# Another order of twelve matrix products: both column halves under one stationary operand, and a tile waited for and released whole

## The chip, the core and the metric

The kernel runs on one core of a Trainium2 chip. The metric is the device time of one execution in microseconds. The kernel before takes 2241.05 us, the median of three runs (2237.48 to 2243.5).

## The reference, cut to what matters

Two transformer layers over 256 tokens of width 1024: an attention mixer, and then a retrieval of experts. The expert part is where the change lies. For each token 8 heads choose 16 of 16384 experts each, and then

```
a   = gelu(sum_d u[e, d] * h[t, d]) * gate[t, e]      # for the chosen experts e of token t
out = sum_e a[t, e] * v[e, :]                         # 256 tokens x 1024
```

The kernel gathers nothing. It computes the product with all 16384 experts, 128 tiles of 128 experts, and the gate is zero where an expert was not chosen. So each layer has an upward pass (h with every tile of `u`) and a downward pass (the weighted activations with every tile of `v`). All of it is in 32-bit floats.

## The kernel before, in words

To keep 32-bit accuracy with TensorE's reduced format, each operand X is split into a high part and a rest, X = hi + lo, and a product is made of three: hi\*hi, hi\*lo, lo\*hi. The work around one tile j of the downward pass is divided so:

- SyncE brings 512 KB of `v` into `raw`, a ring of four (`load_v`, L292), and the 128 KB of stored activations back into `back`, a ring of four that lies in `wmod_ring` (`fetch`, L302). It waits for `lo_done` of the tile four back, and for `al_done` of the tile three ahead of the fetch's own.
- ScalarE makes `hi` of the tile in two instructions, one for each half of 512 columns (`split`, L745), and then `a_hi` of the activations (`split_a`, L773). `hi`, `lo`, `a_hi` and `a_lo` are rings of two, so tile j+2 takes the place of tile j. `split` of half h waits until TensorE has counted up `w_used` for that half of tile j; `split_a` waits for both halves of tile j.
- VectorE multiplies the activations of the tile by the gates (`weigh`, L1082), makes `lo` of both halves (`lower`, L1068), and then `a_lo` (`lower_a`, L1087), in this order, each instruction in the queue behind the one before. In layer 0 it has one more thing to do after `lower_a` of every fourth tile: one of the 32 leftover modulation tiles of layer 1 (`next_modulation`, L1092 and L1095).
- TensorE runs `down(j)`. It waits for `ah_done` and `al_done` (both parts of the activations, whole), and then for each column half h: it waits for `hi_done` and `lo_done` of that half, and for each of two token blocks t it adds three products of 512 columns into bank 2t+h. The twelve products of a tile stand in the order half, token block, product. The twelfth of a half's six counts up `w_used`: the sixth product for half 0, the twelfth for half 1.

The four banks collect sums over all 128 tiles and are read once, after the last. In the code every product goes through the helper `mm`, whose line is L409. A product is two records, a weight load (LDWEIGHTS, engine PEld) and the product itself (MATMUL, engine PE). In the trace `bank<-hi,a_hi` has `a_hi` as the stationary operand and `hi` moving; `bank<-lo,a_hi` has the same stationary operand with `lo` moving; `bank<-hi,a_lo` has `a_lo` stationary.

The pass of layer 0 lies from 816 to 1190 us of the span, that of layer 1 from 1872 to 2220 us.

Of the kernel before, what the change touches and what calls it, by code (L numbers as in the profile page):

```python
# [15 lines left out]
P = 128  # L16
# [3 lines left out]
TT = T // P  # L20
# [17 lines left out]
STREAM = 2 * NKEY  # L38
# [7 lines left out]
HALF = D // 2  # L46
# [62 lines left out]
def build(nc, a, out):  # L109

    with ExitStack() as ctx:
        def sb(name, shape, dt=F32):
            return ctx.enter_context(nc.sbuf_tensor(name, shape, dt))

        def sem(name):
            return ctx.enter_context(nc.semaphore(name))
# [7 lines left out]
        hi = sb("hi", [P, SPLITS, D], F32R)  # L124
        lo = sb("lo", [P, SPLITS, D], F32R)
        a_hi = sb("a_hi", [P, 2, T], F32R)
        a_lo = sb("a_lo", [P, 2, T], F32R)
# [10 lines left out]
        bank = [ctx.enter_context(nc.psum_tensor(f"bank{i}", [P, 512], F32)) for i in range(8)]  # L138
# [112 lines left out]
        s = [{n: sem(f"{n}_{l}") for n in names} for l in range(LAYERS)]  # L251
# [155 lines left out]
        def _(pe):  # L407
            def mm(o, w, x, start=True, stop=True, free=False):
                return nc.tensor.matmul(o, w, x, start=start, stop=stop, skip_group_check=free)  # L409
# [134 lines left out]
            def picks(l):  # L544
                for n in range(4):
                    t, side = n // 2, n % 2
                    pe.wait_ge(s[l]["sel_ready"], 4 * n + 4)
                    c = side * T + t * P
                    for k in range(TOPK):
                        mm(bank[6][:, c:c + P], q_hot[n].rearrange("p h k a -> p (h k) a")[:, :, k], ident, k == 0, k == TOPK - 1)  # L550
                pe.wait_ge(s[l]["pick_ready"], 1)
                for t in range(TT):
                    last = nc.tensor.transpose(bank[7][:, t * P:(t + 1) * P], q_g[:, t].rearrange("p h k -> p (h k)"), ident)
                last.then_inc(s[l]["pick_ps"], 1)

            def experts(l):

                def up(n, r, wait=True):

                    if wait:  # L560
                        pe.wait_ge(s[l]["s_gelu"], n - 1)
                    o = bank[4 + r][:, 0:T]
                    for h in range(2):
                        pe.wait_ge(s[l]["hi_done"], 2 * n + h + 1)
                        pe.wait_ge(s[l]["lo_done"], 2 * n + h + 1)
                        for k in range(h * KT // 2, (h + 1) * KT // 2):
                            c = slice(k * P, (k + 1) * P)
                            mm(o, hi[:, r, c], x_hi[:, k, :], k == 0, False)
                            mm(o, hi[:, r, c], x_lo[:, k, :], False, False)
                            last = mm(o, lo[:, r, c], x_hi[:, k, :], False, k == KT - 1)  # L570
                        last.then_inc(s[l]["w_used"], 1)

                def group(g, b, wait=True):

                    if wait:
                        pe.wait_ge(s[l]["g_copied"], g - 3)
                    pe.wait_ge(s[l]["hot_ready"], g + 1)
                    for n in range(4):
                        last = mm(bank[b][:, n * P:(n + 1) * P], hot[b % 2][:, 0, n, :], hot[b % 2][:, 1, n, :])
                    last.then_inc(s[l]["hot_used"], 1)  # L580

                def down(j, r, first=False, end=False):

                    pe.wait_ge(s[l]["ah_done"], j + 1)
                    pe.wait_ge(s[l]["al_done"], j + 1)
                    for h in range(2):
                        pe.wait_ge(s[l]["hi_done"], STREAM + 2 * j + h + 1)
                        pe.wait_ge(s[l]["lo_done"], STREAM + 2 * j + h + 1)
                        c = slice(h * HALF, (h + 1) * HALF)
                        for t in range(TT):  # L590
                            o, tok = bank[2 * t + h][:, :], slice(t * P, (t + 1) * P)
                            mm(o, a_hi[:, r, tok], hi[:, r, c], first, False, True)
                            mm(o, a_hi[:, r, tok], lo[:, r, c], False, False, True)
                            last = mm(o, a_lo[:, r, tok], hi[:, r, c], False, end, True)
                        last.then_inc(s[l]["w_used"], 1)

                pe.wait_ge(s[l]["xh_done"], 1)
                pe.wait_ge(s[l]["xl_done"], 1)
                up(0, 0, False)
                up(1, 1, False)  # L600
                with pe.Fori(1, GROUP_AT // 2 - 1) as i:
                    for r in range(2):
                        up(2 * i + r, r)
                picks(l)
                for r in range(2):
                    up(GROUP_AT - 2 + r, r)
                for r in range(4):
                    up(GROUP_AT + r, r % 2)
                    group(r, r, False)
                with pe.Fori(1, GROUPS // 4) as i:  # L610
                    for r in range(4):
                        up(GROUP_AT + 4 * i + r, r % 2)
                        group(4 * i + r, r)
                with pe.Fori((GROUP_AT + GROUPS) // 2, NKEY // 2) as i:
                    for r in range(2):
                        up(2 * i + r, r)
                pe.wait_ge(s[l]["g_copied"], GROUPS)
                down(0, 0, first=True)
                with pe.Fori(0, NKEY // 2 - 1) as i:
                    for r in range(2):  # L620
                        down(2 * i + 1 + r, 1 - r)
                down(NKEY - 1, 1, end=True)

            def expert_out(l):
# [9 lines left out]
            for l in range(LAYERS):  # L634
# [4 lines left out]
                if l == 0:  # L639
                    pe.wait_ge(s[0]["sub_sq"], 1)  # L640
                    for n in range(2):
                        last = mm(bank[n][:, :], ones, big[:, n * 512:(n + 1) * 512])
# [678 lines left out]
```

## Time and profile before

| | |
|---|---|
| median of three runs | 2241.05 us (2237.48 to 2243.5) |
| the profiled execution: its time, its span | 2241.37 us, 2239.6 us |
| TensorE products busy | 2083.1 us (93%) |
| VectorE busy | 1490.3 us (67%) |
| ScalarE busy | 1023.9 us (46%) |
| mean granted TensorE clock | 0.96 of full |
| DMA | 447.26 MB, mean 200 GB/s |

How to read the rows further down. A row of a timeline is: start in us from the span's start, duration in us, engine, line, operation, output<-inputs, shapes, count; in brackets the idle time of the engine before it and what ended it. A row of windows is: start:end, length in us, busy us of PE, PEld, DVE, ACT and POOL with instruction counts, the granted TensorE clock, the DMA engines' busy share, GB/s. A row of waits is: who waited for whom, total us, times, longest. In the page's groups: busy us and mean ns of one, then the idle time before them. PE is TensorE's product, PEld its weight load, DVE VectorE, ACT ScalarE, SP SyncE.

### The profile page before, as it was taken

The numbers are of one execution on the slowest core, as the hardware profiler recorded it, in microseconds if no ns is written. First come the engines' busy times: TensorE is split into PE (matmuls) and PEld (weight loads), VectorE is DVE, ScalarE is ACT, GpSimd is POOL, SyncE is SP. The second block draws the span as 40 slices with busy tenths as digits, with TensorE's granted clock in tenths as the row PEclk, the third lists the DMA queues.
The fourth block names the chain that finished last, engine by engine and source line by source line (L and its number), as shares of the span: only waits on it lengthen the run. The fifth ranks groups of instructions, "written<-read, shape, count | busy, mean of one in ns | idle before, by whom it ended". The sixth has DMA issues, their size and how long they took to land.

```text
span 2239.6 us, 43787 instructions
## 1 busy us (share of the span) xinstructions
PE 2083.1 (93%) x12524; PEld 1848.6 (83%) x12524; DVE 1490.3 (67%) x3680; ACT 1023.9 (46%) x2011; POOL 18.7 (1%) x39
## 2 busy tenths in 40 slices
PE   1887689999999999999998889999999999999997
PEld 0755579999999997777777567999999999888886
DVE  5443567875777667887784226785677766777776
ACT  1012124563555555555552222455455555555554
POOL 0000000000000000000000000000000000000000
PEclk7895799999999999999999999999999999999999
DMA  6961344873655688998881213576465568777774
GB/s 238 345 241 44 134 159 134 229 213 105 171 174 173 182 263 303 310 323 305 315 281 44 94 76 113 168 229 180 130 174 173 172 187 248 242 238 242 241 242 152
DMA packets 168453, 447.26 MB, mean 200 GB/s; under 512 B 18625, under 2 KB 85441, under 8 KB 163793
## 3 DMA queue, kind: packets, MB, share of 16 engines
q1 hardware_dynamic: 163472, 393.17, 56.4%
q0 software_dynamic: 4928, 53.45, 6.0%
q8 instruction: 26, 0.43, 0.1%
q14 instruction: 27, 0.21, 0.0%
HBM read 409.84 MB, written 36.70 MB: 199 GB/s over the span
## 4 chain that ended last, share of the span: by engine, by line
PE 88%; DVE 4%; DMA 4%; ACT 2%; issue 1%; SPq 0%; DVEq 0%; ACTq 0%
PE bank L409 87%; DMA raw<-in_v 2%; DMA wmod_ring<-in_w_mod 1%; ACT big L700 1%; PE bank L464 1%; DVE big L906 1%; DVE work L848 0%; DVE wmod_ring L864 0%; ACT hi L745 0%; DVE work L1174 0%; DVE big L970 0%; DVE a_lo L1087 0%; DVE raw L856 0%; DMA c_all<-in_c 0%; PE bank L629 0%
## 5 line engine op out<-in xcount | busy, mean ns | idle before, releaser
L1068 DVE TENSOR_TENSOR lo<-raw,hi 128x512 fp32r<-128x512 f32 x1024 | 702.1, 690 | 375.9 <-ACT hi L745 370.8
L745 ACT ACTIVATE hi<-raw 128x512 fp32r<-128x512 f32 x1024 | 641.8, 629 | 512.2 <-PE bank L409 479.6
L409 PE MATMUL bank<-x_hi,hi 128*128 128x256 f32 x2048 | 590.3, 288 | 1.6 <-ACT work L751 1.6
L409 PE MATMUL bank<-x_hi,lo 128*128 128x256 f32 x2048 | 579.3, 283 | 0.0
L409 PE MATMUL bank<-x_lo,hi 128*128 128x256 f32 x2048 | 579.1, 283 | 0.0
L409 PE MATMUL bank<-hi,a_hi 128*128 128x512 f32 x1024 | 402.9, 393 | 12.3 <-DVE a_lo L1087 9.0
L409 PE MATMUL bank<-lo,a_hi 128*128 128x512 f32 x1024 | 399.9, 391 | 0.0
L409 PE MATMUL bank<-hi,a_lo 128*128 128x512 f32 x1024 | 399.9, 390 | 0.0
L409 PEld LDWEIGHTS bank<-x_hi,hi 128*128 128x128 f32 x2048 | 392.3, 192 | 1.9 <-issue 1.9
L409 PEld LDWEIGHTS bank<-x_lo,hi 128*128 128x128 f32 x2048 | 392.7, 192 | 0.0
L409 PEld LDWEIGHTS bank<-x_hi,lo 128*128 128x128 f32 x2048 | 392.1, 191 | 0.0
L409 PE MATMUL bank<-raw,big 128*128 128x256 f32 (+1 forms) x1248 | 285.7, 390 | 73.6 <-ACT raw L676 58.9
L409 PEld LDWEIGHTS bank<-raw,big 128*128 128x128 f32 (+1 forms) x1248 | 241.9, 195 | 112.7 <-issue 61.2
L409 PEld LDWEIGHTS bank<-hi,a_hi 128*128 128x128 f32 x1024 | 193.0, 188 | 65.6 <-issue 23.0
L409 PEld LDWEIGHTS bank<-hi,a_lo 128*128 128x128 f32 x1024 | 192.9, 188 | 40.8
L409 PEld LDWEIGHTS bank<-lo,a_hi 128*128 128x128 f32 x1024 | 193.1, 189 | 38.9
L751 ACT ACTIVATE work<-bank 128x256 f32<-128x256 f32 x256 | 98.1, 383 | 195.5 <-PE bank L409 194.8
L1076 DVE TENSOR_SCALAR wmod_ring<-cst,wmod_ring 128x128 f32<-128x128 f32 x512 | 142.3, 341 | 0.0
L409 PE MATMUL bank<-wmod_ring 128*128 128x128 f32 x1024 | 135.2, 275 | 0.0
L409 PEld LDWEIGHTS bank<-wmod_ring 128*128 128x128 f32 x1024 | 125.7, 192 | 0.0
L773 ACT ACTIVATE a_hi<-wmod_ring 128x256 fp32r<-128x256 f32 x256 | 103.5, 404 | 10.3 <-DVE wmod_ring L1082 9.5
L1087 DVE TENSOR_TENSOR a_lo<-wmod_ring,a_hi 128x256 fp32r<-128x256 f32 x256 | 107.1, 418 | 0.0
(138 smaller groups left out, 1371.8 us busy)
## 6 DMA issues: line engine op xcount, KB each, us to landing
raw<-in_u SPq DMA_DIRECT2D x256, 512.0 KB, 4.0
raw<-in_v SPq DMA_DIRECT2D x256, 512.0 KB, 4.6
wmod_ring<-in_w_mod SPq DMA_DIRECT2D x96, 512.0 KB, 4.6
s_store<-work SPq DMA_DIRECT2D x256, 128.0 KB, 3.7
wmod_ring<-s_store SPq DMA_DIRECT2D x256, 128.0 KB, 3.6
big<-in_w_in POOLq DMA_DIRECT2D x10, 2048.0 KB, 12.0
big<-in_w_q POOLq DMA_DIRECT2D x16, 1024.0 KB, 6.1
big<-in_w_out POOLq DMA_DIRECT2D x2, 4096.0 KB, 13.1
```

What stands on the lines that cost most here:

```text
L409: return nc.tensor.matmul(o, w, x, start=start, stop=stop, skip_group_check=free)
L464: last = nc.tensor.transpose(bank[4 + n % 2][:, c * P:(c + 1) * P], scores[:, i, c * P:(c + 1) * P], ident)
L700: last = f(c, c, ACT.Exp, bias=neg[:, 2 * i + t:2 * i + t + 1], accum_out=den[:, 2 * i + t:2 * i + t + 1])
L745: f(hi[:, r % 2, c], raw[:, r, c], ACT.Copy).then_inc(s[l]["hi_done"], 1)
L751: f(work[:, r, :], bank[4 + r % 2][:, 0:T], ACT.Gelu).then_inc(s[l]["s_gelu"], 1)
L773: f(a_hi[:, r % 2, :], back[:, b, :], ACT.Copy).then_inc(s[l]["ah_done"], 1)
L906: v.tensor_tensor_reduce(scores[:, i, c], bank[i % 4][:, c], b[:, c], 1.0, -3e38, ALU.add, ALU.max, mx[:, 2 * i + t:2 * i + t + 1]).then_i ...
L1068: v.tensor_tensor(lo[:, r % 2, c], raw[:, r, c], hi[:, r % 2, c].bitcast(F32), ALU.subtract).then_inc(s[l]["lo_done"], 1)
L1076: ins = v.tensor_scalar(hot[r % 2][:, 1, n, :], iota, pick[:, 1, bass.ds(4 * g + n, 1)], pick[:, 2, bass.ds(4 * g + n, 1)], ALU.is_equal, ...
L1087: v.tensor_tensor(a_lo[:, r % 2, :], back[:, b, :], a_hi[:, r % 2, :].bitcast(F32), ALU.subtract).then_inc(s[l]["al_done"], 1)
```

## The change

In `down`, the loop over column halves becomes the innermost one. TensorE now waits once for a tile, for both halves of `hi` and `lo`. For each token block it goes through the three products, and for each of them through both halves: four products in a row have `a_hi` as the stationary operand and two have `a_lo`, and neighbours write to different banks. `w_used` is still counted up twice in a tile, for half 0 by the eleventh product and for half 1 by the twelfth. Number, shapes and operands of the products stay, and so does all that the other engines do.

```diff
                     pe.wait_ge(s[l]["ah_done"], j + 1)
                     pe.wait_ge(s[l]["al_done"], j + 1)
-                    for h in range(2):
-                        pe.wait_ge(s[l]["hi_done"], STREAM + 2 * j + h + 1)
-                        pe.wait_ge(s[l]["lo_done"], STREAM + 2 * j + h + 1)
-                        c = slice(h * HALF, (h + 1) * HALF)
-                        for t in range(TT):
-                            o, tok = bank[2 * t + h][:, :], slice(t * P, (t + 1) * P)
-                            mm(o, a_hi[:, r, tok], hi[:, r, c], first, False, True)
-                            mm(o, a_hi[:, r, tok], lo[:, r, c], False, False, True)
-                            last = mm(o, a_lo[:, r, tok], hi[:, r, c], False, end, True)
-                        last.then_inc(s[l]["w_used"], 1)
+                    pe.wait_ge(s[l]["hi_done"], STREAM + 2 * j + 2)
+                    pe.wait_ge(s[l]["lo_done"], STREAM + 2 * j + 2)
+                    halves = [slice(h * HALF, (h + 1) * HALF) for h in range(2)]
+                    for t in range(TT):
+                        tok = slice(t * P, (t + 1) * P)
+                        o = [bank[2 * t + h][:, :] for h in range(2)]
+                        for h in range(2):
+                            mm(o[h], a_hi[:, r, tok], hi[:, r, halves[h]], first, False, True)
+                        for h in range(2):
+                            mm(o[h], a_hi[:, r, tok], lo[:, r, halves[h]], False, False, True)
+                        for h in range(2):
+                            last = mm(o[h], a_lo[:, r, tok], hi[:, r, halves[h]], False, end, True)
+                            if t == TT - 1:
+                                last.then_inc(s[l]["w_used"], 1)
```

## Rows read from the trace of the kernel before

**Rows 1.** The page: TensorE and VectorE busy; the chain by line.

```profile
PE 2083.1 (93%) x12524; PEld 1848.6 (83%) x12524; DVE 1490.3 (67%) x3680; ACT 1023.9 (46%) x2011; POOL 18.7 (1%) x39
...
PE bank L409 87%; DMA raw<-in_v 2%; DMA wmod_ring<-in_w_mod 1%; ACT big L700 1%; PE bank L464 1%; DVE big L906 1%; DVE work L848 0%; DVE wmod_ring L864 0%; ACT hi L745 0%; DVE work L1174 0%; DVE big L970 0%; DVE a_lo L1087 0%; DVE raw L856 0%; DMA c_all<-in_c 0%; PE bank L629 0%
```

**Rows 2.** Windows: the downward pass of layer 0, then that of layer 1.

```profile
816.49:1189.93 373.44, 361.09 (x1538) 287.49 (x1536) 294.69 (x606) 201.32 (x381) 3.69 (x7) 0.99 0.87 297
1872.10:2220.45 348.35, 348.35 (x1538) 288.21 (x1536) 259.82 (x507) 199.44 (x381) 0.00 (x0) 1.00 0.77 237
```

**Rows 3.** The page's groups: the second product and its weight load.

```profile
L409 PE MATMUL bank<-lo,a_hi 128*128 128x512 f32 x1024 | 399.9, 391 | 0.0
...
L409 PEld LDWEIGHTS bank<-lo,a_hi 128*128 128x128 f32 x1024 | 193.1, 189 | 38.9
```

**Rows 4.** Timeline of layer 1: a tile's end and what it releases.

```profile
2010.39 0.39 PE L409 MATMUL bank<-lo,a_hi 128*128 128x512 f32 x1
...
2010.62 0.39 PE L409 MATMUL bank<-hi,a_lo 128*128 128x512 f32 x1
...
2010.85 0.39 PE L409 MATMUL bank<-hi,a_hi 128*128 128x512 f32 x1
...
2011.05 0.63 ACT L745 ACTIVATE hi<-raw 128x512 fp32r<-128x512 f32 x1 [0.73 <-PE bank L409]
2011.07 0.39 PE L409 MATMUL bank<-lo,a_hi 128*128 128x512 f32 x1
...
2011.58 0.40 ACT L773 ACTIVATE a_hi<-wmod_ring 128x256 fp32r<-128x256 f32 x1
2011.71 0.69 DVE L1068 TENSOR_TENSOR lo<-raw,hi 128x512 fp32r<-128x512 f32 x1 [0.67 <-ACT hi L745]
...
2012.32 0.42 DVE L1087 TENSOR_TENSOR a_lo<-wmod_ring,a_hi 128x256 fp32r<-128x256 f32 x1
2012.40 0.63 ACT L745 ACTIVATE hi<-raw 128x512 fp32r<-128x512 f32 x1 [0.42 <-PE bank L409]
```

**Rows 5.** Timeline of layer 0, after a late transfer: both halves back to back.

```profile
1101.59 1.15 ACT L745 ACTIVATE hi<-raw 128x512 fp32r<-128x512 f32 x2 [4.19 <-DMA raw<-in_v]
1102.25 1.29 DVE L1068 TENSOR_TENSOR lo<-raw,hi 128x512 fp32r<-128x512 f32 x2 [3.38 <-ACT hi L745]
...
1103.46 0.41 DVE L1087 TENSOR_TENSOR a_lo<-wmod_ring,a_hi 128x256 fp32r<-128x256 f32 x1
```

**Rows 6.** Timeline of layer 0, around one modulation tile.

```profile
1070.27 0.39 PE L409 MATMUL bank<-hi,a_lo 128*128 128x512 f32 x1
...
1071.97 0.42 DVE L1087 TENSOR_TENSOR a_lo<-wmod_ring,a_hi 128x256 fp32r<-128x256 f32 x1
...
1072.30 1.22 DVE L1092 CUSTOM_DVE_ANT_0 wmod_ring<-wmod_ring,c_all 128x1024 f32<-128x1024 f32 x1
...
1074.27 1.29 DVE L1068 TENSOR_TENSOR lo<-raw,hi 128x512 fp32r<-128x512 f32 x2
...
1075.47 0.42 DVE L1087 TENSOR_TENSOR a_lo<-wmod_ring,a_hi 128x256 fp32r<-128x256 f32 x1
...
1075.71 0.39 PE L409 MATMUL bank<-hi,a_lo 128*128 128x512 f32 x1
...
1076.21 0.19 PEld L409 LDWEIGHTS bank<-hi,a_hi 128*128 128x128 f32 x1 [0.54 <-issue]
1076.24 0.47 PE L409 MATMUL bank<-hi,a_hi 128*128 128x512 f32 x1
...
1076.55 0.40 PE L409 MATMUL bank<-lo,a_hi 128*128 128x512 f32 x1
```

**Rows 7.** Line L1092 of VectorE, whole span: its instructions.

```profile
L1092 DVE CUSTOM_DVE_ANT_0 wmod_ring<-wmod_ring,c_all x32: 1215/1219/1222, 826.5 to 1186.2; 128x1024 f32<-128x1024 f32 x32
```

**Rows 8.** Waits in the downward pass of layer 0.

```profile
ACT hi L745 <- DMA raw<-in_v: 27.6, 14, 4.2
PEld bank L409 <- issue: 23.0, 32, 2.9
```

## The prediction

> **What bounds the kernel now.** I read the page first: TensorE is busy 93% of the span, and 87% of the chain that ended last is the helper line of the products [rows 1]. So a change to the products' order is on the path as far as it changes how closely they follow each other. Then the two downward passes by windows. Both have 1536 products; layer 1 needs 348.35 us for them and TensorE is busy in all of it, layer 0 needs 373.44 us [rows 2]. Layer 1 thus gives the bare pace: 348.35 / 1536 = 0.2268 us a product, 2.72 us a tile of twelve. Layer 0 loses 25.1 us against that pace. Its waits tell where: 32 times the weight load comes late (23.0 us), 14 times ScalarE had waited for a `v` transfer [rows 8].
>
> **The pace of the products.** The trace shows neighbours of several kinds. The step from `hi,a_hi` to `lo,a_hi` keeps stationary operand and bank: 2010.85 to 2011.07. The step from `lo,a_hi` to `hi,a_lo` changes the operand in the same bank: 2010.39 to 2010.62. The step from `hi,a_lo` to `hi,a_hi` changes operand and bank: 2010.62 to 2010.85 [rows 4]. All are 0.22 to 0.23 us. Keeping the operand alone brings nothing, and a weight load is recorded for every product all the same (1024 for `lo,a_hi`, whose operand is already there) [rows 3]; another bank alone brings nothing either. The change makes a kind that the trace doesn't have, same operand and other bank together. At the full clock (2.4 GHz, granted 1.00) 512 columns are 0.2133 us, so at best 0.0135 us a product is to be had, at worst some small loss. I take 0, the value of all neighbours that are there.
>
> The Trainium skill, page "TensorE: Matmul & The Clock Gate", section "Back-to-back issue gap", gives a warm gap of N/2.4 + 2.5 ns, which is 216 ns for 512 columns. This trace stands 11 ns above it at the full clock. If the new order brought the products to that gap, the estimate by the page would be about 2236 us.
>
> **The wait for the whole tile.** It costs nothing. The old code let half 0 start early only in appearance: before its first product TensorE waits for `a_lo` of the tile, and VectorE makes `a_lo` behind `lo` of both halves. When `a_lo` is there, all is. TensorE also checks as many semaphores before the first product as before; the two checks in the middle of a tile go, and they were hidden by queued products.
>
> **The release of the whole tile.** This is the cost. Call P the start of a tile's last product. Now (all [rows 4]): ScalarE does `hi` half 1 at P + 0.43 (2011.05 against 2010.62), VectorE `lo` half 1 at P + 1.09, `a_lo` at P + 1.70, done at P + 2.12. Half 0 was released six products sooner and done by then. The first product of the tile after next is due at P + 13 x 0.2268 = P + 2.95.
>
> After the change half 0 is released by the eleventh product, one pace before P, so `hi` half 0 starts at P + 0.43 - 0.23 = P + 0.20, and from there everything runs in a row. A late transfer shows what such a row takes: `hi` at 1101.59, both halves without a gap, both `lo`, and `a_lo` over at 1103.87, 2.28 to 2.29 us [rows 5]. So `a_lo` is done at P + 2.49, 0.37 later than now. From its end to the product takes, where TensorE really waits, 0.32 to the weight load and 0.03 more (1075.89, 1076.21, 1076.24); that first product is then stretched, 0.47 instead of 0.39 and 0.31 instead of 0.23 to the next, another 0.08 [rows 6]. Sum P + 2.49 + 0.43 or 0.44 = P + 2.93, against P + 2.95 due. In an undisturbed tile the cover just suffices, with 0.02 us left of now 0.40. Layer 1 (127 such steps) therefore keeps 2.72 us a tile: cost 0. If the cover failed by x, only x/2 a tile would be lost, since two chains of alternate tiles share the engines: (2.93 + x + 11 x 0.2268) / 2. I keep for it 0 to 0.05 us a tile.
>
> **The modulation tiles of layer 0.** Here no cover is left now. VectorE does the 1.22 us reduction, a copy and `weigh` right behind `a_lo`, then two `lo` and the next `a_lo`: `a_lo` starts at 1071.97, the next one at 1075.47, 3.50 us without a hole that matters. TensorE's last product before it starts at 1075.71, the next was due at 1075.94 and comes at 1076.24: 0.30 us lost, plus the stretching [rows 6]. The VectorE chain hangs on the first `a_lo`, which after the change ends 0.37 later, and ScalarE is not in the way (`hi` of the next tile is due at P + 2.92 at the latest, VectorE gets to its `lo` at P + 4.00 + 0.37). The whole 0.37 arrives at TensorE. There are 32 reductions [rows 7]; the last has no tile behind it. 31 x 0.37 = 11.5 us. The restart after the stall is paid already today.
>
> **The transfers.** `load_v` waits for `lo` half 1, now done at P + 1.78, then at P + 2.17: it is issued 0.38 later in a tile. But half 0 of the tile that needs it also starts 1.13 later (P + 0.20 instead of P - 0.93), so in layer 1 the time for landing grows. In layer 0 a transfer hurts only when it lands so late that `a_lo` is late; that point moves with P, and the issue moves 0.38 against it, while four tiles with a modulation in them take 0.37 longer. These cancel: as many late transfers, at the same price. The fetch of the activations is issued and used 0.37 later, cover unchanged. I take 0; six tiles 0.37 later each would be +2.2 us, and less crowded transfers (297 GB/s now, DMA engines 87% busy [rows 2]) could give back 3 us.
>
> **Sum.** 0 (pace) + 0 (wait) + 0 (layer 1) + 11.5 (layer 0) = +11.5 us. Against the profiled execution, 2241.37 us (span 2239.6): 2252.9. That execution is 0.3 above the median, so 2252.6 us against 2241.05.
>
> **Rivals.** (a) *Every tile waits.* The 0.02 us are less than the spread of what I added up. If the undisturbed chain is 0.1 too long, because a weight load that cannot be prefetched costs more than the 0.08 counted (a stall costs its next products a few hundredths more), then 0.04 to 0.05 us is lost in 127 steps of layer 1 and in some 60 of layer 0, two in a group of four: +8 us, 2261; at 0.1 us a tile 2270. For: the thin cover. Against: the layer 1 rows repeat to 0.01 us, and the sum falls on the right side.
>
> (b) *Not slower: the pace falls.* If the 0.0135 us above the bare columns needs both the same bank and a reload, the new order removes it. With all of it gone, layer 1 is then bound by the release chain: (2.93 + 11 x 0.2133) / 2 = 2.64 us a tile, 0.081 x 127 = 10.3 us gained. In layer 0 the stretch from P to the late tile is VectorE's and stays; 23 of 48 products in a group gain, 0.31 x 31 = 9.6 us. 2252.6 - 19.9 = 2232.7. If only the six half-to-half steps of a tile gain, about half: 2243. The point from which it decides is 0.008 us a product on average. For: the combination is untried here. Against: each of its two parts alone changes nothing, and each product still has its weight load. The gap of the page cited above lies inside this case.
>
> (c) *The later release is hidden.* It would need VectorE not to be the bound in the modulation tiles; 2241 to 2245. Against: the lost 0.30 us are there already and VectorE stands right before them.
>
> **How the numbers follow.** Forecast 0.62 (2248 to 2257 with the transfers), (a) 0.17, (b) 0.12 (a third of it at the far end), (c) and the rest 0.09. A change under 0.3%, 6.7 us, cannot be told from none, so slower begins at 2247.8 and faster ends at 2234.3: slower 0.80, same 0.14, faster 0.06. The range leaves out the far ends of (a) and (b): 2243 to 2264.
>
> **What would show it.** In layer 1 the pass should stay at 348 us with products 0.2268 us apart; ScalarE's two `hi` of a tile should start 0.54 us apart, the first 0.43 after the eleventh product; `a_lo` should end at P + 2.49. In layer 0 the gap before the tile behind a modulation should be 0.37 us longer, 31 times, and the pass 385 us. A pace of 0.22 or below, or a pass of layer 1 longer than 350 us, would make the forecast wrong, in (b)'s or (a)'s way.

## The result: 11 us slower, as forecast

The changed kernel takes 2253.07 us (median of five runs, 2250.19 to 2256.1). The kernel before took 2241.68 us beside it (five runs). The ratio is 1.0051, 95% interval 1.0036 to 1.0067. Forecast were 2252.6 us, within 2243 to 2264. The profiled execution took 2253.07 us, with a span of 2251.3 us.

The page of the changed kernel, busy shares and chain by line. They answer to [rows 1] and show next to nothing of the change: TensorE is busy 93% of the span in both.

```profile
PE 2086.3 (93%) x12524; PEld 1841.1 (82%) x12524; DVE 1475.5 (66%) x3680; ACT 997.4 (44%) x2011; POOL 18.8 (1%) x39
...
PE bank L409 85%; DMA raw<-in_v 2%; DMA wmod_ring<-in_w_mod 1%; ACT hi L749 1%; ACT big L704 1%; PE bank L464 1%; DVE lo L1072 1%; DVE big L910 1%; DVE a_lo L1091 0%; DVE wmod_ring L868 0%; DVE wmod_ring L1096 0%; DVE work L852 0%; DVE big L974 0%; DVE work L1178 0%; DVE raw L860 0%
```

The two passes by windows, as in [rows 2]:

```profile
816.14:1197.96 381.82, 361.42 (x1538) 283.77 (x1536) 290.31 (x606) 188.36 (x381) 3.71 (x7) 1.00 0.85 291
1881.20:2232.13 350.93, 350.93 (x1538) 283.92 (x1536) 248.94 (x507) 185.27 (x381) 0.00 (x0) 1.00 0.77 235
```

Layer 0's pass grew from 373.44 to 381.82 us, 8.4, and layer 1's from 348.35 to 350.93, 2.6. The rest of the program holds the other 0.7 of the 11.7 us between the two profiled executions.

A tile of layer 1 in the changed kernel, by timeline (answers to [rows 4]). A row with x2 covers two instructions, and its time is that of both:

```profile
2009.61 0.62 PE L409 MATMUL bank<-hi,a_lo 128*128 128x512 f32 x2
...
2010.03 1.15 ACT L749 ACTIVATE hi<-raw 128x512 fp32r<-128x512 f32 x2 [1.29 <-PE bank L409]
...
2010.06 0.63 PE L409 MATMUL bank<-hi,a_hi 128*128 128x512 f32 x2
...
2010.53 0.62 PE L409 MATMUL bank<-lo,a_hi 128*128 128x512 f32 x2
2010.70 1.29 DVE L1072 TENSOR_TENSOR lo<-raw,hi 128x512 fp32r<-128x512 f32 x2 [0.79 <-ACT hi L749]
...
2010.99 0.62 PE L409 MATMUL bank<-hi,a_lo 128*128 128x512 f32 x2
...
2011.44 0.62 PE L409 MATMUL bank<-hi,a_hi 128*128 128x512 f32 x2
...
2011.91 0.42 DVE L1091 TENSOR_TENSOR a_lo<-wmod_ring,a_hi 128x256 fp32r<-128x256 f32 x1
...
2012.35 0.62 PE L409 MATMUL bank<-hi,a_lo 128*128 128x512 f32 x2
...
2012.65 0.35 PEld L409 LDWEIGHTS bank<-hi,a_hi 128*128 128x128 f32 x2
...
2012.81 0.63 PE L409 MATMUL bank<-hi,a_hi 128*128 128x512 f32 x2
```

The eleventh and the twelfth product start at 2009.61 and 2009.83; the latter is P. `hi` starts 0.42 after the eleventh, at P + 0.20, and both halves follow one another. `a_lo` ends at 2012.33, P + 2.50 (forecast 2.49). The weight load comes 0.32 later. The product starts at P + 2.98: 0.03 over the due P + 2.95, where the forecast had it ready at P + 2.93. It follows its own neighbour (2012.58) by 0.229 us, though, which is 2 ns over the pace. Nearly all of the 0.03 was lost in the tile between: its first pairs start 0.47, 0.46 and 0.45 us after each other (2010.06, 2010.53, 2010.99, 2011.44) where two products at the pace take 0.453, and by the trace five of its products start up to 9 ns late each.

A modulation tile of layer 0 (answers to [rows 6]):

```profile
1075.28 0.42 DVE L1091 TENSOR_TENSOR a_lo<-wmod_ring,a_hi 128x256 fp32r<-128x256 f32 x1
...
1075.61 1.22 DVE L1096 CUSTOM_DVE_ANT_0 wmod_ring<-wmod_ring,c_all 128x1024 f32<-128x1024 f32 x1
...
1077.57 1.29 DVE L1072 TENSOR_TENSOR lo<-raw,hi 128x512 fp32r<-128x512 f32 x2
...
1078.41 0.61 PE L409 MATMUL bank<-hi,a_lo 128*128 128x512 f32 x2
...
1078.78 0.42 DVE L1091 TENSOR_TENSOR a_lo<-wmod_ring,a_hi 128x256 fp32r<-128x256 f32 x1
...
1079.52 0.30 PEld L409 LDWEIGHTS bank<-hi,a_hi 128*128 128x128 f32 x2 [0.92 <-ACT hi L749]
1079.55 0.70 PE L409 MATMUL bank<-hi,a_hi 128*128 128x512 f32 x2 [0.52 <-ACT hi L749]
```

From `a_lo` to the next `a_lo` it is 3.50 us, to the hundredth as before. The last product starts at 1078.64 (0.23 after its neighbour in the x2 row), the next was due at 1078.87 and comes at 1079.55: 0.68 us lost instead of 0.30. The row puts the wait down to ScalarE's `hi`, which had long been done; by the times it is `a_lo`, 0.35 before the product.

### The profile page after: what moved, and what is told of

Read it like the earlier page. It is cut to its first block, busy times and chain, and to the rows that moved or that the text cites. A ratio compares the mean times of both kernels' runs of the same rounds, so it can differ in the third digit from the quotient of the medians.

```text
span 2251.3 us, 43279 instructions
## 1 busy us (share of the span) xinstructions
PE 2086.3 (93%) x12524; PEld 1841.1 (82%) x12524; DVE 1475.5 (66%) x3680; ACT 997.4 (44%) x2011; POOL 18.8 (1%) x39
## 4 chain that ended last, share of the span: by engine, by line
PE 86%; DVE 5%; DMA 4%; ACT 2%; issue 2%; DVEq 0%; SPq 0%; ACTq 0%
PE bank L409 85%; DMA raw<-in_v 2%; DMA wmod_ring<-in_w_mod 1%; ACT hi L749 1%; ACT big L704 1%; PE bank L464 1%; DVE lo L1072 1%; DVE big L910 1%; DVE a_lo L1091 0%; DVE wmod_ring L868 0%; DVE wmod_ring L1096 0%; DVE work L852 0%; DVE big L974 0%; DVE work L1178 0%; DVE raw L860 0%
## 5 line engine op out<-in xcount | busy, mean ns | idle before, releaser
L1072 DVE TENSOR_TENSOR lo<-raw,hi 128x512 fp32r<-128x512 f32 x1024 | 684.0, 689 | 402.3 <-ACT hi L749 396.9
L749 ACT ACTIVATE hi<-raw 128x512 fp32r<-128x512 f32 x1024 | 615.3, 626 | 548.8 <-PE bank L409 520.1
L409 PE MATMUL bank<-hi,a_hi 128*128 128x512 f32 x1024 | 320.7, 394 | 20.4 <-DVE a_lo L1091 13.6
L409 PE MATMUL bank<-lo,a_hi 128*128 128x512 f32 x1024 | 317.4, 391 | 0.0
L409 PE MATMUL bank<-hi,a_lo 128*128 128x512 f32 x1024 | 317.1, 391 | 0.0
L409 PEld LDWEIGHTS bank<-hi,a_hi 128*128 128x128 f32 x1024 | 182.8, 188 | 80.0 <-issue 26.7
L1086 DVE TENSOR_TENSOR wmod_ring<-wmod_ring,big 128x256 f32<-128x256 f32 x256 | 107.3, 420 | 0.3 <-DMA wmod_ring<-s_store 0.3
```

What stands on the lines that cost most here:

```text
L749: f(hi[:, r % 2, c], raw[:, r, c], ACT.Copy).then_inc(s[l]["hi_done"], 1)
L1072: v.tensor_tensor(lo[:, r % 2, c], raw[:, r, c], hi[:, r % 2, c].bitcast(F32), ALU.subtract).then_inc(s[l]["lo_done"], 1)
L1086: v.tensor_tensor(back[:, b, :], back[:, b, :], gates[:, bass.ds(j, 1), :].rearrange("p a t -> p (a t)"), ALU.mult)\
```

## The experiments

All ran against the kernel before, which gave medians of 2239.8 to 2242.4 us beside them. Single executions of one kernel spread by some 10 us. The profiles (one for each kernel) show two places that move without cause in the change: the first pass starts anywhere between 809 and 816 us, and the late transfers of layer 0 cost several us more or less. So beside each ratio stand the passes of the profiled execution, and a value that no late transfer touches: of the thirty groups of four tiles in layer 0, each with one modulation, 19 are free of late transfers, and the starts of their first products in the trace give the mean length of a group. Bare it would be 10.88 us.

| kernel | ratio (95%) | layer 0's pass | group over 10.88 | layer 1's pass |
|---|---|---|---|---|
| before | | 373.4 | 0.37 | 348.35 |
| changed | 1.0051 (1.0036 to 1.0067) | 381.8 | 0.75 | 350.93 |
| release only | 1.0058 (1.0042 to 1.0074) | 385.9 | 0.74 | 351.03 |
| wait only | 1.000 (0.9988 to 1.0012) | 375.9 | 0.36 | 348.35 |
| banks only | 0.9991 (0.9979 to 1.0004) | 375.5 | 0.36 | 348.35 |
| release by the tenth | 1.0016 (1.0002 to 1.003) | 381.6 | 0.51 | 348.35 |
| release by the twelfth | 1.0124 (1.0106 to 1.0141) | 389.5 | 0.97 | 363.00 |
| modulation cut, old order | 0.9974 (0.9963 to 0.9985) | 367.0 | 0.00 | 348.35 |
| modulation cut, new order | 0.9999 (0.9986 to 1.0012) | 371.2 | 0.10 | 351.21 |

### Release only

```diff
-                            mm(o, a_hi[:, r, tok], lo[:, r, c], False, False, True)
+                            late = mm(o, a_hi[:, r, tok], lo[:, r, c], False, False, True)
                             last = mm(o, a_lo[:, r, tok], hi[:, r, c], False, end, True)
-                        last.then_inc(s[l]["w_used"], 1)
+                    late.then_inc(s[l]["w_used"], 1)
+                    last.then_inc(s[l]["w_used"], 1)
```

> The old order of products and the old waits; only half 0's count of w_used moves from the sixth to the eleventh product. Theory (the later release is the whole cost): a_lo ends 0.37 us later after the start of a tile's last product (2.49 instead of 2.12), the gap behind each modulation tile grows by 0.37 us, layer 1 by 0.02 us a tile as in the changed kernel: 2253 us, +11.4 over the kernel before. Rival (the new order of products itself costs, through operand or bank): 2242 us, no change.

Measured: 2253.32 us. Its passes by windows:

```profile
812.92:1198.82 385.90, 363.36 (x1538) 285.39 (x1536) 290.27 (x606) 188.46 (x381) 3.70 (x7) 0.99 0.83 287
1881.50:2232.53 351.03, 351.03 (x1538) 283.93 (x1536) 248.73 (x507) 185.25 (x381) 0.00 (x0) 1.00 0.74 235
```

Layer 1's 351.03 us is the changed kernel's 350.93, and the groups are the same to 0.01 us. By the medians it costs 13.5 us where the changed kernel costs 11.4, with intervals that overlap. The old order with the late release costs what the changed kernel costs, as far as these runs can tell: the release is the whole of it.

### Wait only, and banks only

The first puts both waits of the tile ahead of the loop over halves, with the old order and release. The second keeps waits and release and only turns the products within a half:

```diff
-                        for t in range(TT):
-                            mm(...a_hi, hi...); mm(...a_hi, lo...); mm(...a_lo, hi...)
+                        for t in range(TT): mm(...a_hi, hi...)
+                        for t in range(TT): mm(...a_hi, lo...)
+                        for t in range(TT): mm(...a_lo, hi...)
```

> The old order and the old release; only the wait for both halves of hi and lo before the first product. Theory: 0 us, since a_lo, waited for anyway, is made behind both lo: 2242 us, layer 1's pass stays 348 us. Rival (the coarser wait costs): half 1 comes up to 0.6 us later than half 0, so up to 0.3 us a tile in the late tiles of layer 0, 31 of them: 2251 us.

> Old waits and old release; inside each half the two token blocks take turns, so that all neighbours are in different banks, and no neighbours share the stationary operand. Theory: the pace of products stays 0.2268 us, 2242 us. Rival (the bank matters, one way or the other): a pace that is 0.01 us off moves the sum by up to 15 us either way, 2227 or 2257 us, and shows in layer 1's pass.

Measured: 2239.74 and 2238.44 us, beside 2239.78 of the kernel before. Layer 1's pass is that of the kernel before to the hundredth, first with the whole wait, then with all neighbours in different banks:

```profile
1873.46:2221.81 348.35, 348.35 (x1538) 288.13 (x1536) 259.82 (x507) 199.43 (x381) 0.00 (x0) 1.00 0.75 237
```

```profile
1870.89:2219.24 348.35, 348.35 (x1538) 288.11 (x1536) 259.87 (x507) 199.34 (x381) 0.00 (x0) 1.00 0.76 237
```

### Release one product sooner, or one later

Both start from the changed kernel. The first ends the second token block with half 0, half 0, half 1, half 1, so that the tenth product releases half 0. The second lets the twelfth count for both:

```diff
-                            if t == TT - 1:
-                                last.then_inc(s[l]["w_used"], 1)
+                        if t == TT - 1:
+                            last.then_inc(s[l]["w_used"], 2)
```

> The changed kernel, but in the second token block the last four products go half 0, half 0, half 1, half 1, so that half 0 is released by the tenth product, one product sooner. Theory: a_lo ends at P + 2.27 instead of P + 2.49; layer 1 gets its cover back (348.0 us instead of 350.5), in layer 0 the gap behind a modulation tile is 0.15 us longer than in the kernel before, 31 times: 4.6 us, 2246.5 us in all, 6.5 under the changed kernel. Rival (the order of products costs): near 2253 us, as nearly all neighbours are those of the changed kernel.

> The changed kernel, but the twelfth product counts w_used up by two, so that half 0 is released one product later still. Theory: a_lo ends at P + 2.72 and the tile after next can start at P + 3.16, where P + 2.95 is due; two chains share the engines, so layer 1 takes (3.16 + 11 x 0.2268) / 2 = 2.83 us a tile, 0.107 x 127 = +13.6 us (pass 361.5 us); in layer 0 the VectorE chain behind each modulation is 0.60 later than in the kernel before, 31 times: +18.6 us. Sum +32: 2272 us. Rival (the whole lateness counts, not half): layer 1 +0.21 x 127 = +27 us, sum +45: 2285 us. Rival (the order costs, not the release): near 2253 us.

Measured: 2245.1 us (before: 2239.78) and 2266.88 us (before: 2240.5). Layer 1's pass, released by the tenth and then by the twelfth:

```profile
1877.22:2225.57 348.35, 348.35 (x1538) 288.12 (x1536) 248.82 (x507) 185.30 (x381) 0.00 (x0) 1.00 0.75 237
```

```profile
1882.97:2245.97 363.00, 363.00 (x1538) 278.52 (x1536) 248.67 (x507) 185.27 (x381) 0.00 (x0) 1.00 0.73 227
```

The first is the pace of the new order with its cover back: ten of twelve products stand as in the changed kernel and the pass is the old 348.35 us. So the pair that the trace of the kernel before lacked, same operand and other bank, is worth nothing, and rival (b) is out. The second confirms that only half of a lateness counts where two chains alternate: 363.00 - 348.35 = 14.7 us was measured, 13.6 forecast by halves, 27 by the whole. In layer 0 the groups stand 0.15, 0.38 and 0.61 us (unrounded means) above those of the kernel before for the tenth, eleventh and twelfth; worked out beforehand were 0.15, 0.37 and 0.60. The sum of the second missed (+26 us instead of +32). Its passes are 30.7 us longer than those of the kernel before; its first pass began 5.2 us earlier than in the profile of before, for reasons outside the change.

### The modulation cut in two

`next_modulation` becomes three parts, behind `a_lo` of three successive tiles: the reduction over columns 0 to 511, that over 512 to 1023, and the sum of both.

```diff
+                def next_modulation(part, n, i, r):
+                    c = slice(part * HALF, (part + 1) * HALF)
...
+                    if part < 2:
+                        ins = v.tensor_tensor_reduce(wmod_ring[:, r, c], wmod_ring[:, r, c], c_all[:, c], 1.0, 0.0, ALU.mult, ALU.add,
+                                                     tile_sum[:, part:part + 1])
...
+                    if part == 2:
+                        dve.wait_ge(s[1]["mod_tile"], n + 1)
+                        v.tensor_tensor(mod[1][:, bass.ds(n, 1)], tile_sum[:, 0:1], tile_sum[:, 1:2], ALU.add).then_inc(s[1]["mod_kept"], 1)
```

> The kernel before, but the modulation reduction of VectorE is cut in two of 512 columns each (about 0.7 us with its read-out), behind a_lo of two successive tiles, and the sum of the two is taken in a third. Theory (VectorE's 3.50 us chain is the bound in these tiles): 0.7 us fits into VectorE's spare time in each tile, the stalls of 0.2 and 0.3 us and their restarts of 0.1 us go, 31 x 0.35 = 11 us gained: 2229 us, up to 2234 if more late transfers take a part back. Rival (those tiles wait for something else, a transfer or ScalarE): within 2 us of the kernel before, 2240 us.

> The same cut of the modulation in the changed kernel. Theory: the later release costs nearly only through the modulation tiles; a half reduction behind a_lo at P + 2.08 ends before the next lo is due (P + 2.08 + 0.33 + 0.7 + 0.34 = P + 3.5 against P + 3.58), so the stalls of 0.5 to 0.7 us go, and what is left over the split kernel before is 0.02 us in each of 250 tiles: 2234 us, 5 above it instead of 11 to 13. Rival (the cost is per tile, in the order or in the release): still 11 us or more above the split kernel before, 2241 us or more.

Measured: 2234.85 us for the old order and 2241.4 us for the new, beside 2240.5. Waits in layer 0's pass with the old order (answers to [rows 8]):

```profile
PEld bank L409 <- issue: 13.9, 5, 4.9
PE bank L409 <- DVE a_lo L1087: 11.9, 5, 4.5
```

Of 32 late weight loads 5 are left (before tiles 18, 34, 35, 50 and 98), and the groups without late transfers are at the bare 10.88 us: the chain on VectorE was the bound there. With the stalls gone the new order is 6.6 us behind the old one (5 expected), no longer 11 to 13. Both kernels came out slower than expected, though: the old order gained 6 us instead of 11, and the new one's 2241.4 us is the rival's number, reached because both kernels stand 6 to 7 us higher than expected. What was not gained went into the transfer stalls, which cost the profiled execution 18.7 us, against some 14 in the kernel before. That TensorE, no longer held up elsewhere, met them sooner is my reading; no run isolates it. (The profiled execution of the old order is also its fastest, 2227.39 us: its first pass starts at 809 us.)

### What those five stalls are

In the kernel before, the late transfers stop TensorE before tiles 18, 34, 51, 70 and 98, and in most of the kernels above at these places or one tile beside them. GpSimd's issues in the kernel before, by timeline (the first column is the time; the brackets say that it waited for VectorE's `weigh`), and TensorE after the last stall:

```profile
855.40 0.53 POOL L388 DMA_DIRECT2D big<-in_w_in  x1 [525.46 <-DVE wmod_ring L1082]
903.22 0.53 POOL L388 DMA_DIRECT2D big<-in_w_in  x1 [47.30 <-DVE wmod_ring L1082]
949.92 0.53 POOL L388 DMA_DIRECT2D big<-in_w_in  x1 [46.17 <-DVE wmod_ring L1082]
962.14 0.53 POOL L388 DMA_DIRECT2D big<-in_w_in  x1 [11.69 <-DVE wmod_ring L1082]
1007.15 0.53 POOL L388 DMA_DIRECT2D big<-in_w_in  x1 [44.48 <-DVE wmod_ring L1082]
1021.43 0.53 POOL L388 DMA_DIRECT2D big<-in_w_in  x1 [13.76 <-DVE wmod_ring L1082]
...
1089.76 0.53 POOL L392 DMA_DIRECT2D big<-in_bias  x1 [67.80 <-DVE wmod_ring L1082]
...
1104.27 0.76 PE L409 MATMUL bank<-hi,a_hi 128*128 128x512 f32 x1 [2.53 <-DVE a_lo L1087]
1104.83 0.63 PE L409 MATMUL bank<-lo,a_hi 128*128 128x512 f32 x1
1105.25 0.63 PE L409 MATMUL bank<-hi,a_lo 128*128 128x512 f32 x1
```

These are loads for layer 1: four of 2 MB, the bias maps of 3 MB at 1089.76, and two of 512 KB at 962.14 and 1021.43. Some 12 us behind each large one (15 behind the third) TensorE stands for a late `v` tile; no stall stands 12 us behind the two small ones. Two of the stalls also cost TensorE its clock: behind the last one, after 2.5 us without a product, the granted clock is 0.50 (1.2 GHz) from 1104.27 to 1106.96 and products are 0.42 us apart instead of 0.23. Before tile 70 the same holds for part of 1021.2 to 1024 (granted 0.65). Three kernels with the old order tried this. *Spread loads*: 18 pieces of 512 KB, one in six tiles, and the bias maps (`in_bias`) at the end of the pass. *Spread and split*: the same with the modulation cut; also for the new order. *Spread all*: bias maps in pieces as well, 24 pieces, one in five tiles.

```diff
-                        pool.wait_ge(s[0]["a_ready"], -(-e // T))
-                    pool.dma_start(big[:, b:e], w[:, b:e]).then_inc(win_in[n], 16)
+                        for p in range(b, e, D):
+                            pool.wait_ge(s[0]["a_ready"], 6 * (p // D + 1))
+                            pool.dma_start(big[:, p:p + D], w[:, p:p + D]).then_inc(win_in[n], 16)
```

> The kernel before, but GpSimd's prefetch of layer 1's input weights (five loads of up to 2 MB, issued as the downward pass of layer 0 frees their place) goes in 18 pieces of 512 KB, one every six tiles, and the 3 MB of bias maps is issued at the end of the pass instead of in it. Theory (the late transfers of layer 0, always before tiles 18, 34, 50, 70 and 98, are v tiles held up by those loads, issued some tiles before each): these five stalls with their half-clock restarts, about 14 us, go: 2227 us, pass of layer 0 near 360 us. Rival (the late transfers come from the modulation loads or from the sum of traffic): the stalls move to other tiles, 2237 to 2241 us.

> The kernel before with both edits: the modulation cut in two, and the weight loads in pieces. Theory: nothing is left of the 25 us that layer 0's pass stood above layer 1's: pass 348 to 352 us, 2217 us in all. Rival (the transfers of layer 0, now at some 325 GB/s, become the bound): 2225 us or more.

> The changed kernel with both edits. Theory: with the modulation stalls gone the later release costs only its 0.02 us a tile, in both layers: 5 us above the old order with the same edits, 2222 us. Rival (the release costs per stall, of whatever kind): no stalls are left, so no difference; or (the order costs) 11 us above it.

> The kernel before with the modulation cut in two, and with the weight loads and the bias maps of layer 1 all in 512 KB pieces, 24 of them, one every five tiles of layer 0's downward pass. In the run with the bias at the end both passes were at the bare 347.96 us, but the stretch between them had grown from 682.6 to 690.8 us, as the reload of x stood behind the 3 MB. Theory: that comes back, 8 us, and both passes stay at 348 us: 2214 us. Rival (at 891 KB a tile, 327 GB/s, the transfers of layer 0 become the bound): the pass grows again by 8 us or more, 2222 us.

| kernel | median, before beside it | ratio (95%) |
|---|---|---|
| spread loads | 2233.51, 2242.41 | 0.9955 (0.994 to 0.9971) |
| spread and split | 2222.35, 2242.41 | 0.9917 (0.9901 to 0.9932) |
| spread and split, new order | 2228.22, 2242.41 | 0.9935 (0.9918 to 0.9953) |
| spread all | 2210.95, 2240.12 | 0.9878 (0.9856 to 0.99) |

With the loads alone spread, layer 0's pass stands 11.4 us above the bare one, which is 31 times the 0.37 of the modulation groups; no stall by a transfer is left:

```profile
813.87:1173.64 359.77, 356.65 (x1538) 285.69 (x1536) 295.58 (x606) 202.93 (x381) 10.07 (x19) 1.00 0.88 302
```

The passes of spread and split, then of the new order with the same edits:

```profile
812.05:1160.40 348.35, 348.35 (x1538) 288.11 (x1536) 295.31 (x670) 199.16 (x381) 10.07 (x19) 1.00 0.91 312
1850.76:2199.11 348.35, 348.35 (x1538) 288.11 (x1536) 259.88 (x507) 199.47 (x381) 0.00 (x0) 1.00 0.77 237
```

```profile
815.77:1167.22 351.45, 351.45 (x1538) 284.09 (x1536) 291.90 (x670) 185.30 (x381) 10.02 (x19) 1.00 0.90 308
1857.86:2208.98 351.12, 351.12 (x1538) 283.99 (x1536) 248.97 (x507) 185.25 (x381) 0.00 (x0) 1.00 0.76 235
```

Now both passes of the old order are bare, and the new order costs 3.1 and 2.8 us, 5.9 us by the medians. All 25 us that layer 0's pass stood above layer 1's are named: late modulation tiles and late `v` tiles. The three kernels with the bias maps at the end came out 5 to 7 us above what was expected of them. The stretch between the passes shows why: it grew from 682.2 to 690.4 us in spread and split, as the reload of `x` stood behind the 3 MB. The chain of waits of spread and split shows it:

```profile
1156.44 11.80 DMA raw<-x_store
```

Spread all puts that right (the stretch is 682.4 us again), at 2210.95 us (2214 expected), 1.2% under the kernel before and the fastest of all. Layer 0's pass keeps its pace there at 319 GB/s but for 0.3 us:

```profile
810.51:1159.14 348.63, 348.63 (x1538) 287.93 (x1536) 294.61 (x670) 198.53 (x381) 12.67 (x24) 1.00 0.91 319
```

## Why the prediction was right, step by step

**The pace, 0.** Right. Layer 1's pass in the old order, in the banks-only order and in the mostly new order of the tenth-product kernel is 348.35 us in each. The trace shows 0.2268 us a product for all of them, 11 ns above the 216 ns that the Trainium skill ("TensorE: Matmul & The Clock Gate", section "Back-to-back issue gap") gives for 512 columns. The page means that figure for an isolated product, which the prediction did not say, and names 131 ns for a stream of them; no order tried here reached either.

**The whole wait, 0.** Right, by the wait-only kernel. TensorE waited for `a_lo` anyway.

**The whole release, cover of 0.02 us left in an undisturbed tile, cost 0.** Not quite right. `a_lo` ends where it was put, within 0.01 us, and the tile's first product is hardly held up: over the 127 steps of layer 1 it follows its neighbour after 0.229 us on average, 2 ns over the pace. The forecast counted a late weight load only as far as it holds up that first product. The load comes 0.07 us behind its usual place (2012.65, where it would stand at 2012.58), and then the next five products start up to 9 ns late each. In the kernel before no load is late in layer 1 and no such row of slow starts is there. Why a late load slows the products behind it stays open. It adds up to 0.02 us a tile, 2.6 us in layer 1 instead of 0. The prediction had named a pass of layer 1 over 350 us as the sign of rival (a), every tile waits, and it came: 350.93 us. So rival (a) is true in a small form, 2.6 us in layer 1 and 0.6 in layer 0 where it had put 8 in all.

**The modulation tiles, 31 x 0.37.** Right. A group grew by 0.38 us, which is 11.8 us in 31: 0.36 in the late tile and the one behind it (11.2 us), and 0.02 in the two undisturbed tiles (0.6 us). Cutting the modulation removes the stall in both orders; 0.10 a group is left in the new one, 0.02 to 0.03 in each of its four tiles, as in layer 1.

**The transfers, cancelling.** The places of the late transfers stayed for the most part. Their sizes vary by several us between executions: layer 0's pass was 381.8 us in the changed kernel and 385.9 with the release alone, while the undisturbed groups agree within 0.01 us. So in the profiled pair the transfers gave back some 3 us. The closeness of 2252.6 to 2253.07 is partly luck: those 3 us, for which the forecast had 0, nearly made up for the 2.6 and 0.6 us of the undisturbed tiles, for which it also had 0. Layer 0's pass, forecast at 385 us, measured 381.8. That layer 0's 14 us of transfer stalls come from GpSimd's large loads I had not seen; the forecast did not need it.

**Rival (c), a hidden release.** Out: the stalls grew by the full amount.

## What to carry to other kernels

When a release moves to the end of a tile, lay out the row of work that hangs on it and compare its end with the moment the buffer is due. A ring of two leaves one tile of time (here until P + 2.95), and the work of ScalarE and VectorE in a row ended at P + 2.50, with the weight load at P + 2.82, 0.07 us behind its usual place. Where such a cover is thin, an extra task on a producer's queue that already causes stalls passes on the whole delay. Cutting that task into pieces that fit the spare time of several tiles gained 6 us here, more than any order of the products that was tried. Large prefetches beside a stream that needs most of the bandwidth (DMA engines 87% busy here) did better in pieces of 512 KB, spread over the stage and not left to its end, where the next stage's first load stands behind them.

## What the runs showed of the hardware that I had not expected

A weight load that comes 0.07 us late did not hold up its own product by more than some 2 ns, but the five products behind it started up to 9 ns late each, 0.02 us in all, before the stream was back at its pace. And with layer 1's weight loads in pieces of 512 KB, layer 0's pass held its bare 348.35 us at 91% busy DMA engines and 312 GB/s, and with the bias maps in such pieces too it missed that by 0.3 us at 319 GB/s; with loads of 2 and 3 MB among them and 297 GB/s the kernel before lost up to 2.9 us at once, the wait-only kernel up to 4.8 us at 295 GB/s.
